# Two fillers of 96 bytes in the on-chip memory of a one-core transformer step, so that large buffers begin at multiples of 128 bytes

## What is computed

```python
m = jnp.split(jax.nn.silu(cond) @ w_mod + b_mod, 6, axis=-1)       # modulation, w_mod 2048 x 12288
h = rms_norm(y, norm_mix) * (1 + m[1]) + m[0]
q, k, v, u = jnp.split(h @ w_in, [1024, 2048, 3072], axis=-1)      # w_in 2048 x 4096
att = neighbourhood_attention(q, k, v, cache_k, cache_v, rpb)      # latents; plain attention for the context
mix = jnp.concatenate([att, pool_mixer(u, w_pool, pool_scale)], axis=-1) @ w_out
y = y + m[2] * mix
h = rms_norm(y, norm_ffn) * (1 + m[4]) + m[3]
g, idx = lax.top_k(softmax(h @ w_router, over tokens), cap)        # 16 experts, 128 latent + 32 context tokens each
ys = (silu(xs @ w_gate) * (xs @ w_up)) @ w_down * g                # xs = the chosen tokens
y = y + m[5] * scatter_add(ys)
return rms_norm(y, norm_final)                                     # and new_k, new_v
```

## Time and profile before

| | us |
|---|---|
| median of 3 runs | 4052.84 |
| lowest and highest | 4049.37 to 4055.34 |
| the profiled execution | 4056.79 |
| its span, first to last instruction | 4055.2 |
| TensorE busy in the span | 3808.7 (94%) |
| VectorE, ScalarE, GpSimd busy | 2462.2 (61%), 1774.5 (44%), 455.7 (11%) |

### The profile page before, as it was taken

One profiled execution on the slowest core, in us unless ns is written; L12 is line 12 of the kernel. 1 busy time (PEld: TensorE's weight loads), 2 busy tenths in 40 slices (PEclk: granted clock), 3 DMA queues, 4 the chain that ended last, 5 costly groups with the idle time before them and its releaser, 6 DMA issues. The chain is left out here.

```text
span 4055.2 us, 67855 instructions
## 1 busy us (share of the span) xinstructions
PE 3808.7 (94%) x24856; PEld 3365.5 (83%) x24856; DVE 2462.2 (61%) x4721; ACT 1774.5 (44%) x2654; POOL 455.7 (11%) x473
## 2 busy tenths in 40 slices
PE   7899999999799999899998699999999999999992
PEld 3688888888688888799998588888888888988881
DVE  4655555555366666332332777777777777777774
ACT  3611111111167776311113566666655665665653
POOL 0000000000165554000000100000000000000000
PEclk9999999999899999899999799999999999999996
DMA  9544344444465654644525588887777887887876
GB/s 348 160 131 135 125 130 133 131 130 131 134 185 156 191 155 149 231 136 152 188 81 212 190 259 265 261 260 253 262 260 256 269 271 251 270 264 260 269 245 250
DMA packets 572187, 825.46 MB, mean 204 GB/s; under 512 B 23552, under 2 KB 458176, under 8 KB 560320
## 3 DMA queue, kind: packets, MB, share of 16 engines
q1 hardware_dynamic: 548448, 700.96, 52.9%
q0 software_dynamic: 23648, 123.25, 9.4%
HBM read 717.20 MB, written 108.00 MB: 203 GB/s over the span
## 5 line engine op out<-in xcount | busy, mean ns | idle before, releaser
L2020 DVE TENSOR_TENSOR e_wlo<-e_raw,e_whi 128x1024 fp32r<-128x1024 f32 x768 | 905.3, 1219 | 331.0 <-ACT e_whi L1939 328.0
L2157 PE MATMUL ps<-e_xs,e_whi 128*128 128x320 f32 x4096 | 1055.5, 344 | 10.5 <-DVE e_xs L2034 6.9
L2157 PE MATMUL ps<-e_xs,e_wlo 128*128 128x160 f32 x4096 | 935.0, 238 | 0.0
L1939 ACT ACTIVATE e_whi<-e_raw 128x1024 fp32r<-128x1024 f32 x768 | 766.0, 1049 | 288.9 <-DMA e_raw<-in_w_up 125.8
L2157 PEld LDWEIGHTS ps<-e_xs,e_wlo 128*128 128x128 f32 x4096 | 770.8, 191 | 0.6
L2157 PEld LDWEIGHTS ps<-e_xs,e_whi 128*128 128x128 f32 x4096 | 753.5, 188 | 14.9 <-issue 7.9
L2175 PE MATMUL ps<-e_whi,e_h 128*128 128x512 f32 x1024 | 403.8, 394 | 1.5 <-DVE e_h L2060 1.4
L489 PE MATMUL ps<-hhi,p_whi 128*128 128x512 f32 (+1 forms) x1536 | 386.7, 360 | 8.4 <-DVE p_wlo L428 8.4
L446 DVE SCALAR_TENSOR_TENSOR p_acc<-p_modraw,cT,p_acc 128x256 f32<-128x256 f32 x960 | 386.5, 478 | 0.5 <-DMA p_modraw<-in_w_mod 0.5
L489 PE MATMUL ps<-hlo,p_whi 128*128 128x512 f32 (+1 forms) x1536 | 383.4, 358 | 0.0
L489 PE MATMUL ps<-hhi,p_wlo 128*128 128x512 f32 (+1 forms) x1536 | 383.1, 358 | 0.0
(11 more groups left out here) (255 smaller groups left out, 5504.2 us busy)
## 6 DMA issues: line engine op xcount, KB each, us to landing
e_raw<-in_w_gate SPq DMA_DIRECT2D x64, 2048.0 KB, 8.2
e_raw<-in_w_up SPq DMA_DIRECT2D x64, 2048.0 KB, 8.2
e_raw<-in_w_down SPq DMA_DIRECT2D x64, 2048.0 KB, 8.0
p_modraw<-in_w_mod SPq DMA_DIRECT2D x128, 512.0 KB, 3.6
m_raw<-in_w_mod SPq DMA_DIRECT2D x16, 2048.0 KB, 14.9
p_raw<-in_w_in SPq DMA_DIRECT2D x64, 512.0 KB, 4.8
o_raw<-in_w_out SPq DMA_DIRECT2D x16, 2048.0 KB, 8.6
projT<-p_out_st POOLq DMA_DIRECT2D x32, 640.0 KB, 3.2
```

The source lines that it names most:

```text
L1939: nc.scalar.activation(piece(whi, c, q), piece(raw, c, q), ACT.Copy).then_inc(w_hi_made, 1)
L2020: nc.vector.tensor_tensor(piece(wlo, c, q), piece(raw, c, q), piece(whi, c, q).bitcast(F32), ALU.subtract).then_inc(w_lo_made, 1)
L2157: last = nc.tensor.matmul(bank[:, 0:cols], w[:, s, at:at + P], xs[:, k, 0:cols], start=(k == 0 and w is whi), stop=(k == KD - 1 and w is whi))
```

## The change

Three things are edited. Two tensors that no instruction uses are allocated, 24 words (96 bytes) of each partition: fill_left between nfT and mulT, and fill_right at the top of the right stack. SB_TOP, from which the places of hhi and hlo are counted, goes down by the same 96 bytes. And the two index tables of the router grow from 17 words to 32, so that idxL, idxC, gL and gC together take 384 bytes and not 320. No instruction is added or removed, and the order on every engine stays the same.

```diff
@@ -51,7 +51,7 @@
 CH = 4096
 CW = CH // KD
 AHEAD = 1
-SB_TOP = 229344
+SB_TOP = 229248
 H_ROW = TOK * 4
@@ -86,6 +86,8 @@
         ones = sb("ones", [P, 1])
         nmT = sb("nmT", [P, KD])
         nfT = sb("nfT", [P, KD])
+        sb("fill_left", [P, 24])
+        top.enter_context(nc.sbuf_tensor("fill_right", [P, 24], F32, side="right"))
         mulT = sb("mulT", [P, 2, KD])
         addT = sb("addT", [P, 2, KD])
@@ -96,8 +98,8 @@
         output_projection(nc, sem, locals())
         with ExitStack() as route:
             top_route = route
-            idxL = route.enter_context(nc.sbuf_tensor("idxL", [P, E + 1], U32))
-            idxC = route.enter_context(nc.sbuf_tensor("idxC", [P, E + 1], U32))
+            idxL = route.enter_context(nc.sbuf_tensor("idxL", [P, 32], U32))
+            idxC = route.enter_context(nc.sbuf_tensor("idxC", [P, 32], U32))
             gL = route.enter_context(nc.sbuf_tensor("gL", [P, E], F32))
             gC = route.enter_context(nc.sbuf_tensor("gC", [P, E], F32))
             gate_row = route.enter_context(nc.sbuf_tensor("e_gate_row", [P, 2, D], F32))
```

## The result

The changed kernel takes 4033.57 us (median of 5 runs, 4028.18 to 4034.97), beside 4054.4 us (4049.37 to 4055.84, 5 runs) for the kernel before: a ratio of 0.995 with a 95% interval of 0.9936 to 0.9963. A second set on another chip gave 4038.56 (4030.12 to 4041.8, 4 runs) beside 4057.72: 0.9946 (0.9926 to 0.9965). So it is 19 to 21 us faster.

A forecast was written before the change was run, and what follows sets the result against it. The prediction took TensorE to bound the kernel (busy 3,808.7 of 4,055.2 us), with transfers or router steps in some 325 us; matmuls, weight loads, VectorE/ScalarE and transfers were each put at 0, giving 4,053 us, range 4,041 to 4,063.

## What to carry to other kernels

Count the places of buffers within 256 bytes, not 128: where 1,024-byte rows are loaded and the loads are waited for, begin the buffer at a multiple of 256, and expect some 9% off the packet time (measured here for this one size of row). Then look at the distance between loaded weights and streamed rows as a second, separate setting, to be tried for each form of matmul: it was worth 1% of the projections, and the same 128 bytes cost 0.4 to 0.5% in gate and up. And a comparison of two bad cases that agree says nothing on the good one: build the good one, or leave the whole bound in the range.

## What the runs showed of the hardware

- Packets of 1,024 bytes from HBM into the on-chip memory: 46.6 to 46.8 ns at a multiple of 256 in the opening, 50.9 to 51.3 at any of five other places, 128 among them. In the experts: 47.2 to 47.5 at 0, 50.0 to 50.4 elsewhere.
- Three matmuls of 512, 512 and 256 columns per weight block: 587 ns with weights and streamed rows 0 or 64 bytes apart within 256, 580 with 128 or 192 (384 reads as 128); at 160 and 224 the steps vary and their means are 580.0 and 581.5. Matmuls of 256 columns, by the count in 100 us: 119.6 ns at 0 and 118.3 at 128. Pairs of 320 and 160 columns: 256.6 at 0 and 257.8 at 128. Why the distance counts, and why the sign turns, was not found; other distances were not tried in the last two.
- Loads of weights in the input projection and in gate and up (188 ns, those of e_wlo 191) moved by no more than 1 ns in any kernel; those of the output projection took 192 to 193 ns at distance 0 and 189 at 128. VectorE's operations stayed within 1 to 3 ns (1,219 to 1,220 for e_wlo, 1,225 to 1,226 for p_wlo, 1,217 to 1,220 for o_wlo, 689 for L1757).
